# Output products ahead of two norms in two passes over the tokens, latent first, then context

## What is computed

```python
x = x + gt1 * out_lat                                   # attention output product (att_w_out)
x = x + gt2 * conv_ffn(modulate(rmsnorm(x, norm2_g[layer]), sh2, sc2), ...)
...
def rmsnorm(x, g):
    y = xf * lax.rsqrt(jnp.mean(xf * xf, axis=-1, keepdims=True) + EPS)
def conv_ffn(h, w_up, conv_w, conv_b, w_down):
    gate, val = jnp.split(jnp.dot(h, w_up), 2, axis=-1)
    return jnp.dot(jax.nn.silu(dwconv(gate, conv_w, conv_b)) * val, w_down)
```

## Time and profile before

| | before |
|---|---|
| device time, median of 3 runs | 2638.74 us (2637.91 to 2642.46) |
| span of the profiled execution | 2637.0 us |
| the profiled execution's own device time | not given apart; the median of the runs is 1.7 us above the span |
| PE busy | 2447.8 us, 93% |
| DVE busy | 1559.3 us, 59% |
| ACT busy | 952.0 us, 36% |
| POOL busy | 201.0 us, 8% |
| granted TensorE clock, mean | 0.968 of full speed |

### The profile page before, as it was taken

One profiled execution on the slowest core, in us unless ns is written; L12 is line 12 of the kernel. 1 busy time (PEld: TensorE's weight loads), 2 busy tenths in 40 slices (PEclk: granted clock), 3 DMA queues, 4 the chain that ended last, 5 costly groups with the idle time before them and its releaser, 6 DMA issues.

```text
span 2637.0 us, 33653 instructions
## 1 busy us (share of the span) xinstructions
PE 2447.8 (93%) x13706; PEld 1959.8 (74%) x13706; DVE 1559.3 (59%) x2452; ACT 952.0 (36%) x1707; POOL 201.0 (8%) x157
## 2 busy tenths in 40 slices
PE   4998898989999999989999889999989989989997
PEld 2875565678888888868886767877768866858765
DVE  4256678648766775665426578877753246364464
ACT  3355556523212121234234332322343135343352
POOL 1000001002101011100001011111100000000010
PEclk8999999999999999989999899999989989999999
DMA  6232100023333332212120144444312120112301
GB/s 234 88 117 92 41 1 1 9 88 104 116 131 102 131 110 98 96 56 64 57 86 4 50 146 160 158 166 144 130 62 64 59 74 1 49 40 80 116 1 64
DMA packets 65995, 223.62 MB, mean 85 GB/s; under 512 B 7216, under 2 KB 10928, under 8 KB 65072
## 3 DMA queue, kind: packets, MB, share of 16 engines
q1 hardware_dynamic: 63648, 214.65, 24.2%
q10 hardware_dynamic: 2192, 6.82, 0.7%
HBM read 219.34 MB, written 2.10 MB: 84 GB/s over the span
## 4 chain that ended last, share of the span: by engine, by line
PE 82%; DVE 9%; ACT 4%; DMA 3%; POOL 1%; issue 1%; SPq 0%; ACTq 0%; DVEq 0%
PE pair L1092 21%; PE pair L1093 20%; PE pair L1094 20%; PE pair L1259 5%; PE side L1308 3%; DMA RAW<-in_w 2%; PE pair L1295 2%; DVE T L1960 2%; ACT T L1705 1%; PE side L1295 1%; DVE ACC L1949 1%; DVE WL L1807 1%; PE pair L1118 1%; PE pair L768 1%; DVE HL L1968 1%
## 5 line engine op out<-in xcount | busy, mean ns | idle before, releaser
L1092 PE MATMUL pair<-HH,WH 128*128 128x512 f32 (+1 forms) x2496 | 887.3, 355 | 45.9 <-DVE HL L1968 37.0
L1093 PE MATMUL pair<-HL,WH 128*128 128x512 f32 (+1 forms) x2496 | 872.6, 350 | 0.0
L1094 PE MATMUL pair<-HH,WL 128*128 128x512 f32 (+1 forms) x2496 | 871.9, 349 | 0.0
L1807 DVE TENSOR_TENSOR WL<-RAW,WH 128x1024 fp32r<-128x1024 f32 (+4 forms) x286 | 314.1, 1098 | 501.3 <-ACT WH L1407 490.7
L1407 ACT CAST WH<-RAW 128x1024 fp32r<-128x1024 f32 (+4 forms) x286 | 271.4, 949 | 880.2 <-DMA RAW<-in_w 877.2
L1092 PEld LDWEIGHTS pair<-HH,WH 128*128 128x128 f32 x2496 | 478.3, 192 | 131.4 <-DVE HL L1968 48.9
L1094 PEld LDWEIGHTS pair<-HH,WL 128*128 128x128 f32 x2496 | 479.2, 192 | 60.0
L1093 PEld LDWEIGHTS pair<-HL,WH 128*128 128x128 f32 x2496 | 480.0, 192 | 58.6 <-issue 1.2
L1949 DVE SCALAR_TENSOR_TENSOR ACC<-MODW,CVF,ACC 128x512 f32<-128x512 f32 x364 | 324.5, 949 | 0.0
L1092 PE MATMUL pair<-DH,WH 128*128 128x512 f32 (+1 forms) x624 | 228.3, 366 | 11.7 <-POOL DL L2325 9.8
L1093 PE MATMUL pair<-DL,WH 128*128 128x512 f32 (+1 forms) x624 | 221.2, 355 | 0.0
(11 more groups left out here) (318 smaller groups left out, 2554.1 us busy)
## 6 DMA issues: line engine op xcount, KB each, us to landing
RAW<-in_w SPq DMA_DIRECT2D x242, 512.0 KB, 3.5
MODW<-in_w SPq DMA_DIRECT2D x104, 512.0 KB, 4.4
RAW<-in_w SPq DMA_DIRECT2D x48, 384.0 KB, 3.1
RAW<-in_w SPq DMA_DIRECT2D x16, 256.0 KB, 2.6
DFL<-in_dft_lat ACTq DMA_DIRECT2D x4, 1024.0 KB, 7.0
X<-in_x SPq DMA_DIRECT2D x1, 3072.0 KB, 15.6
out_x<-X SPq DMA_DIRECT2D x8, 256.0 KB, 2.0
RAW<-in_w SPq DMA_DIRECT2D x8, 192.0 KB, 2.4
```

The source lines that it names most:

```text
L1092: mm(out[0:j.m, c:e], wh[k], a, start=k == 0, stop=False)
L1093: mm(out[0:j.m, c:e], wh[k], b, start=False, stop=False)
L1094: ins = mm(out[0:j.m, c:e], wl[k], a, start=False, stop=k == j.k - 1)
L1807: TT(WL[:, j.n % NRING, 0:c], RAW[:, j.n % NRING, 0:c], WH[:, j.n % NRING, 0:c].bitcast(F32), ALU.subtract).then_inc(*dve.mark("lo", j.n))
```

## The change

The eight output products ahead of a2 and of b1 become sixteen: eight over the 512 latent tokens (`t0=CTX`), then eight over the 256 context tokens (`t0=0, t1=CTX`), each with its own load of the weights and its own split. The latent squares are summed on PE behind context product 0 (`SUMS_AFTER`), ACT takes the root in stage 0 of context product 1, and the latent features are made in stage 0 of context products 2 to 6, ahead of DVE's epilogue (`FEATURES_AT`; the last two low parts at 7). In the norm phase only the context part is left; its sums stand on PE behind the latent half of held product 0. The two engines no longer wait for each other ahead of these norms. `GROUPS` becomes 4, 6, 6, 6 tiles for both FFNs. Modulation blocks of layer 0 follow every down product of groups 0 to 2 and none of the last.

```diff
-GROUPS = [(0, 6), (6, 12), (12, 18), (18, 22)]
+GROUPS = [(0, 4), (4, 10), (10, 16), (16, 22)]
+SPLIT_NORMS = ("a2", "b1")
+SUMS_AFTER = 0
+FEATURES_AT = {2: (0, 1), 3: (2,), 4: (3, 4), 5: (5,), 6: (6, 7)}
...
-(j.kind == "addx" and (j.more["col"] % 2 or (j.layer == 0 and j.more["step"][2] < 2)))
+(j.kind == "addx" and "part" not in j.more and (j.more["col"] % 2 or (j.layer == 0 and j.more["step"][2] < 3)))
...
+def token_parts():
+    return [dict(part=0, t0=CTX), dict(part=1, t0=0, t1=CTX)]
...
+        for part in token_parts() if b == FT and t0 == 0 else [dict(t0=t0)]:
+            for m in range(KD):
+                down(m, **part)
...
-                          step=("attout", m)) for m in range(KD)]))
+                          step=("attout", m), **part) for part in token_parts() for m in range(KD)]))
...
+        def part_sums(q, s):
+            a, b = (CTX, TOK) if s == 0 else (0, CTX)
+            take(2)
+            pe.wait_ge(*step("nacc", q["id"], KD - 2, s))
+            pe.wait_ge(*step("nsq", q["id"], s, KD - 1))
+            sums_of(s, T[2][:, a:b], T[1][:, a:b], ("nss", q["id"], s))
+            free[2] = [("nrstd", q["id"], s, "ln")]
...
                     if stage == 0 and normed and j is held[0]:
                         job(j, [(512, TOK), (CTX, 512)], last=False)
+                        if state["late"]:
+                            part_sums(state["late"], 1)
...
                         job(j)
+                        if j.sq and j.more.get("part") == 1 and j.sq[1] == SUMS_AFTER:
+                            part_sums(j.sq[0], 0)
...
                             split()
+                        if j.sq and j.more.get("part") == 1:
+                            q, k = j.sq
+                            if k == SUMS_AFTER + 1:
+                                norm_root(q, 0, CTX, TOK)
+                            features_high(q, 0, CTX, TOK, FEATURES_AT.get(k, ()))
...
+            elif j.kind == "addx" and "part" in m:
+                dve.wait_ge(*step("mm", j.n))
+                x = X[:, m["col"], j.t0:j.t1]
+                STT(x, pairs[pr][:, 0:j.t1 - j.t0], modv(m["blk"], m["gate"] + m["col"], m["part"]), x, ALU.mult, ALU.add).then_inc(*dve.mark("psum_read", j.n))
...
+                        if j.sq and j.more.get("part") == 1:
+                            if j.sq[1] == 0:
+                                norm_scales(j.sq[0])
+                            for k in FEATURES_AT.get(j.sq[1], ()):
+                                if k == 0:
+                                    dve.wait_ge(*step("nrstd", j.sq[0]["id"], 0))
+                                feature(j.sq[0], 0, CTX, TOK, k)
+                                if k >= 2:
+                                    feature_low(j.sq[0], 0, CTX, TOK, k - 2)
+                            if j.sq[1] == KD - 1:
+                                feature_low(j.sq[0], 0, CTX, TOK, KD - 2)
+                                feature_low(j.sq[0], 0, CTX, TOK, KD - 1)
                         epilogue(j, uses[0] % 2)
```

More of the change, by code:

```diff
@@ L113, in with_mods @@
             out.append(due.pop(0)[1])
-        room = j.kind == "val" or (j.kind == "gate" and (j.more["i"] % 2 or j.more["g"] == 0)) or (j.kind == "addx" and (j.more["col"] % 2 or (j.layer == 0 and j.more["step"][2] < 2)))
+        room = j.kind == "val" or (j.kind == "gate" and (j.more["i"] % 2 or j.more["g"] == 0)) or (j.kind == "addx" and "part" not in j.more and (j.more["col"] % 2 or (j.layer == 0 and j.more["step"][2] < 3)))
         if room and extra:
@@ L143, in ffn_jobs, with down @@
             out.append(Job("val", "ffn_w_up", layer, KD, [(FF + i * P, P)], t0=t0, i=i, g=g, at=i - a))
-        for m in range(KD):
-            out.append(Job("addx", "ffn_w_down", layer, b - a, [(m * P, P)], row=a * P, t0=t0, col=m,
-                           blk=layer, gate=40, rhs="hid", step=("down", layer, g, m)))
+        def down(m, **tokens):
+            out.append(Job("addx", "ffn_w_down", layer, b - a, [(m * P, P)], row=a * P, base=t0, col=m,
+                           blk=layer, gate=40, rhs="hid", step=("down", layer, g, m), **tokens))
+        for part in token_parts() if b == FT and t0 == 0 else [dict(t0=t0)]:
+            for m in range(KD):
+                down(m, **part)
     return out
@@ L1033, in _ @@
         mm = nc.tensor.matmul
-        state = {"hready": [], "first": False, "columns": False, "low": False}
+        state = {"hready": [], "first": False, "columns": False, "low": False, "late": None}
         def take(bank):
@@ L1085, in job @@
                 rh, rl = HH, HL
-            off = 0 if src == "hl" or (src == "hid" and j.t0) else j.t0
-            n = TOK - j.t0
+            off = 0 if src == "hl" else j.t0 - j.more.get("base", 0)
+            n = j.t1 - j.t0
             for c, e in tokens or [(c, min(n, c + 512)) for c in range(0, n, 512)]:
@@ L1952, in mod_block, with norm_scales @@
                 dve.also("macc", blk, g)
+        def norm_scales(q):
+            dve.wait_ge(*step("mod", q["blk"], q["scale"] + KD - 1))
+            g = PAR[:, PARAMS[q["g"]] + q["gl"] * KD:PARAMS[q["g"]] + (q["gl"] + 1) * KD]
+            for s in range(2):
+                c = modcol(q["blk"]) + 2 * q["scale"] + s
+                dve.wait_ge(*dve.own())
+                STT(AB[:, s, :], MOD[:, c:c + 2 * KD - 1:2], 1.0, g, ALU.add, ALU.mult).then_inc(*dve.mark())
         def feature(q, s, a, b, k):
```

49 lines of the change are left out of this document (33 added, 16 removed).

## The result

The changed kernel is slower: median 2653.81 us (2647.26 to 2660.08, 10 runs) against 2643.27 us of the kernel before (2637.91 to 2652.03, 10 runs beside them), a ratio of 1.0038 [1.0025, 1.0050]. On 2643 us that is +10 us, between +7 and +13. The forecast was 2650.5 us, +11.8 on the span of before, with 0.65 on slower. The three runs known at the time of the forecast had a median 4.5 us under that of the ten, so the difference is the number to compare, not the absolute time. The profiled execution took 2653.68 us, its span is 2652.0 (before 2637.0), its mean granted clock 0.965 (before 0.968).

What follows compares the result with a forecast made beforehand. PE, busy 93% of 2637.0 us, was taken as the bound. Terms 4.2 (a2) + 4.1 (b1) + 2.5 and 1 (groups) = +11.8 gave a span of 2648.8, plus 1.7 for the median: 2650.5 us; range 2636 to 2662.

Steps and rivals of the forecast that it cites:

- rival A: Ahead of a2 and b1, the round DVE-ACT-DVE sets the pace of the context passes; 2650.5 us; chance 0.50.
- (1): Ahead of a2, latent sums wait behind context product 0 for the addition of square 6; PE idles 4.4 us.
- (2): Ahead of a2, sums to the root's start take 3.55 us; context product 1 ends at 13.7 us.
- (3): Ahead of a2, product 1's end frees the slot for product 5: cast at 17.4, split done at 19.8 us.
- (4): Ahead of a2, DVE-ACT-DVE rounds of stages 2 to 6 take 26.3 us against 14.4 of products; low parts done 47.6.
- (5): Ahead of a2, held product 0 may start at 43.0 us, waits for low parts, ends its second piece at 50.9.
- (6): At a2, context sums, root and eight context features reach 60.7 us; held products end at 64.0, before 60.2.
- Rival B1: In stages 2 to 7 DVE does not wait for ACT; 5.4 us off each norm, about 2640 us; chance 0.19.
- Rival B2: Context-pass loads are early too, under about 0.5 us from product's end to cast; about 2625 us; chance 0.13.
- Rival C: PE at 1.2 GHz from context passes through held product 0; 2.9 to 4 us per norm, about 2657; chance 0.16.
- Ahead of b1: Context pass to held products at b1, last group of 6 tiles: end at 61.0 us against 56.9, +4.1 us.
- The groups: Groups 4, 6, 6, 6 in the FFNs: layer 0 +2.5 us from modulation blocks on DVE, layer 1 +1 us.

Runs made afterwards that it cites:

- w1: The changed kernel with DVE's features ahead of the split from stage 2 on (at stage 7 the last two low parts): 0.9986 of the kernel before.
- s0: As a run: the changed kernel again, no edit, for a second trace; 1.0042 of the kernel before.
- t2: The changed kernel with the cast and split of context product 3 one stage later: 0.9990 of the kernel before.
- t3: The changed kernel with the edits of t2 and w1 together: 0.9950 of the kernel before.

## Why the prediction was right, and where it was off

The mechanism, rival A, came as forecast, and the steps of a2 can be laid beside the trace one by one. Time 0 is 556.20.

| step | forecast | trace |
|---|---|---|
| (1) product's end to cast of 3 | 3.7 | 559.88: 3.7 |
| (1) PE idle before the latent sums | 4.4 | 4.53 |
| (2) context product 1 ends | 13.7 | 571.35: 15.1 |
| (3) split of 5 done | 19.8 | 577.1: 20.9 |
| (4) rounds | 5.8, 4.4, 5.2, 5.0, 5.9 | 5.7, 4.2, 5.5, 5.0, 5.75 |
| (4) last low parts done | 47.6 | 604.6: 48.4 |
| (5) held product 0 starts | 43.0 | 600.26: 44.1 |
| (6) end of the held products | 64.0 | 621.3: 65.1 |

- **Step (2), a term that was too small.** I gave the sums the 3.55 us of a time when they had run at the slow level, but product 1 behind them its full speed. It began at 1.2 GHz (steps of 0.21 us instead of 0.12) and ended 1.4 us late. The later steps carry 0.8 to 1.1 of that, so a2 came out at +4.6 us where I had +3.8.
- **Step (6), a sign that did not come.** I named waits for context features of 3 to 5 us in all as a sign. PE has none that the list of waits shows: from 600.30 to 621.30 it is busy 20.86 of 21.00 us, and only held product 0's context half (614.60 to 618.26) takes 0.8 us more than 2.87, at full clock, in short pauses. My own steps left only 0.6 us of idle time there, so the sign contradicted the sum; the sum was near.
- **Rival B1** (DVE does not wait for ACT) is out for this order: DVE idles 2.49, 0.71, 0.46, 2.04 and 1.37 us on casts. But w1 shows how near it lay. One reordering on DVE makes it true and wins about the 5.4 us per norm that I had priced it at (measured 4.7 in the rounds, 6.6 in all). My argument against it, that the cast stands behind the high part in ACT's order, holds in both kernels; what decides is whether DVE has something to do meanwhile.
- **Rival B2** (loads early) is out: 3.7 us from product's end to cast, as in the earlier trace rows.
- **Rival C** (1.2 GHz through held product 0) came only in part: 0.88 in the context pass, 0.92 in the held products. At a2 these slow matmuls cost next to nothing. Those of context products 4 and 6 stand ahead of waits for DVE (0.92 us, and 3.06 one product later). The slow first piece of held product 0 ended at 605.1, and its last low parts were only ready at 604.6. There the rule of the Trainium skill ("TensorE: Matmul & The Clock Gate", What's actually happening), as I had applied it, is not borne out: with PE busy 20.99 of 28.80 us the pass was broken up, and yet not throttled as a whole. For the sums, idle 4.53 us before them and at 0.50 after, the trace agrees with it.
- **Ahead of b1** I forecast 61.0 us against 56.9. The trace has 1220.88 - 1160.9 = 60.0 against 56.7: +3.3 instead of +4.1, with PE idle 4.29 us instead of 4.2 before the sums. In s0 it is 1222.20 - 1159.91 = 62.3, +5.6. There 11 of 18 matmuls of context product 1 and 23 of 24 of held product 0's first latent piece ran at 1.2 GHz. So one trace says it to some 2 us only, and something of rival C can show here.
- **The groups: two wrong terms.** Layer 0, forecast +2.5: without b1 it went from 596.0 - 56.7 = 539.3 to 599.6 - 60.0 = 539.6, +0.3. I had let 4.5 us of DVE work per product stand against 4.2 of PE and added the difference eight times; in the trace PE waits for an update in that FFN only twice, 0.7 us in all. The sign that I gave, down products of group 0 starting 4.5 us apart, came in number only: the seven steps from 680.72 to 713.67 are 4.2 to 5.3 us, but PE is busy 32.21 of these 32.95 us, and the longer steps hold its own sums for the modulation blocks and a few matmuls at 1.2 GHz. Layer 1, forecast +1: 402.8 became 399.8 (s0: 400.8), so -2 to -3, a wrong sign.
- **The sum.** By the traces: +4.6 (a2), +3.6 to +6.2 (layer 0 with b1), -3 to -2 (layer 1), together +5 to +9, against +10 [7, 13] by the medians. My +11.8 came near the latter since the groups' 3.5 us that never came stood in for what the traces leave open. The point estimate is better than its terms.

Between +5 to +9 by the stretches and +10 [7, 13] by the medians there is little to fill, and what fills it is not settled. The 15.0 us between the two spans do add up: 3.2 ahead of the first changed product (509.28 and 512.52), 4.6 in the joint of a2, 3.6 on to b1, -3.0 in layer 1 and 6.6 behind the sums of s0. The first and the last are the same instructions in all kernels. Ahead of the change 508.3 to 515.4 us pass in the 14 traces. From the sums of s0 to the end the trace of before has 705.9 us, that of the change 712.5, and s0, the same kernel, 708.2. This last stretch in before, in t2 and in t3:

```profile
1931.11:2637.00 705.89, 651.16 (x3702) 520.43 (x3702) 325.14 (x575) 271.17 (x527) 30.09 (x28) 0.95 0.16 54
```

```profile
1934.14:2648.20 714.06, 662.47 (x3702) 527.73 (x3702) 325.40 (x575) 270.97 (x527) 30.07 (x28) 0.93 0.16 53
```

```profile
1913.61:2627.90 714.29, 660.90 (x3702) 526.08 (x3702) 325.44 (x575) 271.33 (x527) 30.14 (x28) 0.94 0.15 53
```

The counts are equal, DVE and ACT are equally busy, and PE is busy longer at a lower clock. t3, 13 us faster by its median, has one of the longest of these stretches, so it does not go with the edits. But the trace of before has the shortest of all 14, and it is the only one of that kernel. Between before and the change 6.8 us of difference arise in one place, the third layer's attention. Here are 35 us of it, of the change, then before, then t2:

```profile
2150.00:2185.00 35.00, 33.77 (x133) 19.42 (x134) 18.69 (x63) 14.07 (x61) 0.00 (x0) 0.51 0.09 35
```

```profile
2143.00:2178.00 35.00, 31.56 (x200) 19.37 (x200) 24.03 (x74) 18.31 (x70) 0.00 (x0) 0.86 0.02 8
```

```profile
2142.00:2177.00 35.00, 33.89 (x131) 19.22 (x132) 17.51 (x61) 12.71 (x56) 0.00 (x0) 0.50 0.16 64
```

Column PEclk is 0.51, 0.86 and 0.50; s0 has 0.71. t2, at the low level here, is still level with the kernel before by its median, so this comes and goes with the execution and not with the edit, as far as one trace each can tell. It also warns of comparing spans: t2's span (2648.2) would have said "slower".

## What to carry to other kernels

Splitting a pass in two leaves PE's work alone but shortens the cover over everything done once per product; what was hidden in 8.3 us sticks out of 2.9. Here it was not the amount of added work that made the loss but its place in the in-order queues: look for the instruction that waits for a late transfer, and for what stands behind it that somebody else needs (here a split ahead of the addition that lets PE sum). Put work that others wait for, and work that is ready, ahead of work that still has to wait; two such moves of existing instructions turned a loss of 10 us into a gain of 13.

## What was not expected of the hardware

- An idle time of 4.5 us on PE was followed by 1.2 GHz for the sums and about half of the next product, one of 1.4 us by full speed (first two sum matmuls 2.07 and 1.12 us). So a wait shortened by 3.15 us gave back 5.9 by the start of product 2 and 5.3 at the end of the joint. Shorter waits were not all harmless: in the change's context pass those of 2.00 and 1.89 us were each followed by 17 of 24 matmuls at 1.2 GHz and the one of 0.92 us by none, while after one of 2.01 us in t2 the product ran at full speed.
- DVE's addition of 256 columns takes 0.42 us alone (584.65) and 1.17 while POOL subtracts (589.68; POOL's row runs from 589.28 to 590.56). The Trainium skill ("SBUF — State Buffer", Who interferes with whom) says that a DVE instruction with two inputs in SBUF contends with a GpSimd instruction that reads SBUF; the trace agrees. In one of the forecast's rounds this is 0.75 us that I hadn't put in.
- Code-identical stretches differ by up to 8 us between executions of a one-core kernel (705.9 to 714.7 us for the last 27% of the program). In the traces above the longer ones have the lower granted clock, 0.93 and 0.94 against 0.95, with equal busy times of DVE and ACT.
